# A decode attention stage: the order of TensorE's products within a step

## The reference

```python
s = jnp.einsum('bqhd,bkhd->bhqk', qi, k).astype(F32) * scale
s = s + ci[..., None] - ckt[:, :, None, :]            # cumulative log forget of query and key
s = jnp.where(k_pos[None, :] <= pi[:, None], s, MASK_VALUE)
p = jax.nn.softmax(s, axis=-1).astype(v.dtype)
return jnp.einsum('bhqk,bkhd->bqhd', p, v)
```

## Time and profile before

| | |
|---|---|
| median of 3 runs | 1877.27 us (1875.54 to 1879.39) |
| the profiled execution | 1880.6 us, of which the profile spans 1878.8 us |
| mean granted TensorE clock | 0.991 |
| busy share of the span: PE, DVE, ACT, POOL | 97%, 49%, 37%, 31% |

### The profile page before, as it was taken

The page is one execution under the profiler, slowest core; times in us unless marked ns, Lnnn a source line. Parts: engine busy times, 40 slices in busy tenths (PEclk is TensorE's granted clock), DMA queues, the critical chain, the costliest instruction groups (busy, mean ns, idle before and its releaser), DMA issues. The chain is left out here.

```text
span 1878.8 us, 41127 instructions
## 1 busy us (share of the span) xinstructions
PE 1821.9 (97%) x17185; PEld 1693.8 (90%) x17185; DVE 912.5 (49%) x1398; ACT 694.2 (37%) x1089; POOL 579.6 (31%) x295
## 2 busy tenths in 40 slices
PE   6999998999999999999998999999989999999998
PEld 5999997999999999999996677777779999999998
DVE  4767766245555521145653466655543555554000
ACT  5355455432222222245632455555544122122111
POOL 2323331233333343333531011221114334333332
PEclk9999999999999999999999999999989999999999
DMA  5242232232232232242346999999962222223222
GB/s 121 77 111 82 81 100 66 68 90 79 79 90 79 79 94 83 75 141 71 113 138 230 407 379 387 377 355 360 358 223 80 85 85 79 85 84 96 78 77 82
DMA packets 289101, 273.75 MB, mean 146 GB/s; under 512 B 19602, under 2 KB 250099, under 8 KB 288404
## 3 DMA queue, kind: packets, MB, share of 16 engines
q1 hardware_dynamic: 286980, 268.62, 43.8%
q10 hardware_dynamic: 1792, 1.44, 0.3%
q0 software_dynamic: 144, 1.05, 0.1%
HBM read 254.64 MB, written 16.43 MB: 144 GB/s over the span
## 5 line engine op out<-in xcount | busy, mean ns | idle before, releaser
L1973 POOL TENSOR_TENSOR a_wl<-a_wraw,a_wh 128x1024 fp32r<-128x1024 f32 (+2 forms) x91 | 233.3, 2564 | 400.0 <-ACT a_wh L1897 400.0
L1973 POOL TENSOR_TENSOR b_wl<-b_wraw,b_wh 128x1024 fp32r<-128x1024 f32 (+1 forms) x66 | 172.7, 2616 | 297.8 <-ACT b_wh L1897 297.8
L1854 PE MATMUL ps<-xh,a_wh 128*128 128x288 f32 x1104 | 238.4, 298 | 0.0
L1854 PE MATMUL ps<-xl,a_wh 128*128 128x288 f32 x1104 | 237.1, 296 | 0.0
L1854 PE MATMUL ps<-xh,a_wl 128*128 128x288 f32 x1104 | 236.9, 296 | 0.0
L1897 ACT ACTIVATE a_wh<-a_wraw 128x1024 fp32r<-128x1024 f32 (+2 forms) x91 | 100.6, 1105 | 335.0 <-PE ps L1854 315.4
L1897 ACT ACTIVATE b_wh<-b_wraw 128x1024 fp32r<-128x1024 f32 (+1 forms) x66 | 75.0, 1136 | 318.4 <-PE ps L1854 318.4
L1990 DVE TENSOR_TENSOR xT<-xT,ps 128x576 f32<-128x576 f32 x32 | 24.1, 754 | 321.1 <-PE ps L1854 321.1
L1854 PEld LDWEIGHTS ps<-xh,a_wh 128*128 128x128 f32 x1104 | 177.1, 187 | 1.1 <-issue 0.2
L1854 PEld LDWEIGHTS ps<-xh,a_wl 128*128 128x128 f32 x1104 | 177.3, 187 | 0.6
L1854 PEld LDWEIGHTS ps<-xl,a_wh 128*128 128x128 f32 x1104 | 177.2, 187 | 0.6
(11 more groups left out here) (352 smaller groups left out, 3879.0 us busy)
## 6 DMA issues: line engine op xcount, KB each, us to landing
a_wraw<-in_w_gate_up SPq DMA_DIRECT2D x44, 512.0 KB, 3.8
b_wraw<-in_w_gate_up SPq DMA_DIRECT2D x44, 512.0 KB, 3.8
xT<-in_cache_k SPq DMA_DIRECT2D x40, 512.0 KB, 6.4
xT<-in_cache_v SPq DMA_DIRECT2D x40, 512.0 KB, 6.9
a_wraw<-in_a_w_in SPq DMA_DIRECT2D x32, 512.0 KB, 4.2
f_h_plain<-in_cache_k SPq DMA_DIRECT2D x30, 512.0 KB, 5.9
xl_plain<-in_cache_v SPq DMA_DIRECT2D x30, 512.0 KB, 6.5
f_h_plain<-in_cache_v SPq DMA_DIRECT2D x30, 512.0 KB, 6.5
```

What stands on the lines that cost most here:

```text
L1854: mm = pe.matmul(ps[0:width(n), bank(n) + a, 0:HALF], wt[:, base(n) + t, 0:width(n)], ap[:, first + t, a * HALF:(a + 1) * HALF], start=kin ...
L1973: pool.tensor_tensor(part(wl, n), part(wraw, n), part(wh, n).bitcast(F32), ALU.subtract).then_inc(e["low"], 1)
```

## The change

In each step the scores are issued before the value mixes and the prompt's mix. The decay row, formerly a part of `scores`, becomes a function of its own and is issued last in odd steps. In even steps the signal `scored` is still given by the last score, in odd steps by the decay row.

```diff
-                if half == 1:
-                    if n % SEQ_STEPS == 1:
-                        pe.wait_ge(rload[b % 2], b // 2 * 16 + 16)
-                        pe.wait_ge(e["selected"], 1)
-                    mm = pe.matmul(ps[:, SCORE_BANK, :], rowsel[:, group % G, :], rowr[:, b % 2, :], start=False, stop=True,
-                                   skip_group_check=True)
-                mm.then_inc(e["scored"], 1)
+                if half == 0:
+                    mm.then_inc(e["scored"], 1)
+
+            def decay(n):
+                b, group = n // SEQ_STEPS, n // 2
+                if n % SEQ_STEPS == 1:
+                    pe.wait_ge(rload[b % 2], b // 2 * 16 + 16)
+                    pe.wait_ge(e["selected"], 1)
+                pe.matmul(ps[:, SCORE_BANK, :], rowsel[:, group % G, :], rowr[:, b % 2, :], start=False, stop=True,
+                          skip_group_check=True).then_inc(e["scored"], 1)
...
+                if n < KSTEPS:
+                    scores(n)
                 for m in pages.mixed_at(n):
                     mix(m)
                 if turned is not None:
                     unit_mix(turned)
-                if n < KSTEPS:
-                    scores(n)
+                if n < KSTEPS and n % 2 == 1:
+                    decay(n)
```

## The result

The changed kernel takes 1882.47 us in the median of 19 runs, the kernel before, run beside it, 1878.61. The ratio is 1.0018, with a 95% interval of 1.0011 to 1.0025: slower by 3.4 us (2.1 to 4.7). The forecast was 4.8 us slower, 1882.1 us. The profiled execution of the changed kernel took 1884.15 us, 1882.3 of it in the span.

A forecast was written before the change was run, and what follows sets the result against it. TensorE's program order was taken to set the pace. Stalls of +5.8 us, with -0.3, -1.0, +0.6 and -0.3, gave +4.8 us on 1877.3: 1882.1 us, own range 1881.1 to 1883.5, wider range 1878.7 to 1884.8.

The forecast's parts named there:

- The uncovered steps: Eleven steps from 12 to 63 where no other work covers VectorE's key copy: 0.53 us each, +5.8 us.
- What comes back: Further gains and losses in steps 10 to 63: -0.3, 0, -1.0, +0.6 and -0.3 us.
- Step 10: Scores fill the gap where the mix waits 0.34 us for ScalarE's copy of the probabilities: -0.3 us.
- Step 40: Scores cover the prompt's mix's 0.38 us wait for its copy, but step 41 loses the gain again: 0.
- key waits of steps 49 and 57: Keys wait 0.77 and 0.28 us for ScalarE; the longer steps 48 and 56 take from these waits: -1.0 us.
- the new values' products: In steps 41, 49 and 57 the scores' own 0.09 us falls away behind these products: -0.3 us.
- the passage behind the prompt's mix: Passage to full products at the end of steps with a prompt mix: 0 to 1.2 us, taken as +0.6.
- the passage behind the scores: Sixteen scores ahead of full products: 0.98 us against 0.89 for sixteen mixes ahead of quarter products, a 0.09 us cost.
- Sooner key copies: Rival: earlier scores end the identity loads' 8.5 us of waits for ScalarE's key copies; -3.7 us, 1873.6, chance 0.05.
- Pages: Rival: page transfers by DMA set the pace, so TensorE's new waits add nothing; 1877.3 us, chance 0.07.
- a rival with a shorter drain: Passage behind the prompt's mix costs nothing, as its products stream half the columns; +2.0 us, 1879.3, chance 0.10.
- The clock: Rival: the stage-end half clock stays away, +1.5 us, chance 0.08; or step 41 brings another, +8.1 us, chance 0.07.

The follow-up runs named there:

- seven-step experiment: The changed kernel with scores also ahead of the prompt's scores and the tail in seven further steps; ratio 1.0046 to the kernel before.

## Why the prediction was right, and where a size was off

**The sum and the luck in it.** The time of 1882.47 us lies 0.4 us from the forecast, but the loss is 3.4 us (3.7 in the steps) and not 4.8, and so below the +3.8 that the forecast's own range began with. The two times agree so well because the kernel before took 1878.61 us in 19 runs, where the forecast had started from 1877.3, the median of three: that part is luck. With 19 runs of each kernel the interval is 2.6 us wide, so a loss under the 3.8 us that the prediction took for the limit could still be told from none. The direction and the place of the loss were right, and so was the size of most terms.

**The uncovered steps.** Right in place, number and price: the eleven steps that were listed, and no others from step 10 on. Nine of them grew by 0.51 or 0.52 us where 0.53 was set; steps 41 and 49 hold the same stall among other differences. 11 x 0.52 is 5.7, against 5.8. The experiments show the cause, since the loss goes away with the old order in these steps, with half of the scores behind the mix, and by as much as the copy is shorter with half of the copy.

**What comes back.** Step 10 gave 0.40 us where 0.3 was set. Step 40 gave 0.59, and step 41 lost it again: 0.97 is the new stall of 0.52 and the 0.59, less 0.14. With the old order in step 41, the pair reads -0.59 and +0.59. The key waits of steps 49 and 57 gave 0.51 (0.77 to 0.26) and 0.46 (0.59 less the 0.13 that step 57 saves without it), 1.0 as forecast. Behind the new values' products 0.13 or 0.14 us were saved three times, 0.4 where 0.3 was set.

**The mis-sized term** is the passage behind the prompt's mix. I took +0.6 us, the middle of 0 to 1.2. Most steps with a prompt mix did not change at all, and steps 47 and 61 are 0.09 shorter each. The error lies in the 0.09 us that I set for the passage behind the scores. Step 40 above shows sixteen products of the same shape twice: the first group behind full products takes 0.89 us (1225.65 to 1226.54), the second, behind quarter products, 0.86 (1226.54 to 1227.40). I had taken the 0.89 of a first group as the bare length of the scores, which stood second; so their passage to full products cost 0.98 - 0.86 = 0.12 us and not 0.09. The prompt's mix of step 40 takes 0.99 ahead of transposes (1227.40 to 1228.39) and 0.87 ahead of scores, again 0.12. The two passages cost the same, and the term is nil. The 0.13 or 0.14 that steps 41, 49 and 57 saved is about the same. Without this term the sum would have been 4.2, and with the measured figures for step 10 and the new values 4.0; steps 10 to 63 measured 3.7. The rest is 0.1 in the eleven steps and the 0.2 of steps 47 and 61, which no term had: there the prompt's mix started 0.95 us after the mix ahead of it and starts 0.86 us after it now. That it had waited for its copy, as in step 40, is likely and not shown, since no view names a wait there.

**A reading.** The long stretch of the earlier trace rows, which the prediction takes for steps 11 to 63, ends 0.9 us after step 63 begins. Nothing in the sum hangs on it.

**The rivals.** Sooner key copies did not come: the weight loads' wait for them is 8.2 us in 31 cases, where it was 8.5 in 32. Pages did not become a wait, and the longest landing is 9.1 us, where it was 10.4. The rows of the changed kernel are:

```profile
PEld ps L1261 <- ACT at_kt L1425: 8.2, 31, 1.1
...
DMA to landing us min/median/max: 3.8/6.1/9.1
```

The passages added nothing and saved nothing. By the Trainium skill's rule (TensorEngine Tiling (Array Packing), Tiling Modes) that a change of tiling mode drains the engine, I had made a rival with a shorter drain. The seven-step experiment agrees with the rule itself, 0.32 us for one passage in each direction, but the passage behind the prompt's shorter products is no cheaper: 0.12 us, as behind the scores. The clock stayed full in steps 10 to 63. The half clock at the stage's end lasts as long in both kernels' profiled executions, so it explains none of their difference. That this fall can stay away, as the rival supposed, is shown by four of the experiments (last section).

## What to carry to other kernels

Where one engine issues everything in program order, a group is best put behind other ready work if its inputs come from a copy that has just been asked for; price a reordering by the first place in the same trace where the new neighbours already stand side by side, and count only the steps in which nothing else covers the copy. Then follow each saved or lost half microsecond to the next wait: here a sixth of the loss was given back by a chain that hung on something else, and one gain was lost to it. When a group moves, compare the products on both sides of it, in the old place and in the new.

## What the runs showed of the hardware that was not expected

The fall to half clock in the stage's end does not stand in one place in the profiled executions of these kernels, with the same code there. In the kernel before it covers 1365 to 1372 us, in the changed one 1369 to 1376. In the kernel with the old order in the eleven steps, that stretch is at full clock, and the half clock comes only at the change to the next stage, where the other two have a second stretch of it; three more of the nine show it so:

```profile
1362.00:1375.00 13.00, 11.76 (x142) 8.64 (x145) 7.82 (x24) 6.16 (x17) 0.00 (x0) 1.00 1.03 403
1383.60:1393.50 9.90, 4.33 (x18) 4.36 (x19) 5.42 (x9) 4.73 (x9) 2.33 (x1) 0.50 0.48 144
```

A single execution's span therefore can't tell kernels apart here that differ by a few microseconds, while the lengths of the steps ahead of it can.

TensorE's products need not start in program order. In step 63 of the kernel with scores on both sides of the mix, one product of the mix starts at 1355.29 us, ahead of three scores that stand before it in the program and start from 1355.31 on. In no other step from 10 to 63 of any of these kernels does a mix overtake scores or the reverse.
